# A two-layer streaming encoder step on one core: residuals written straight to SBUF, weight splits and norm rows in another order, another end

## The reference, cut to what matters

```
for each of 2 layers, for 256 prompt rows and 32 sample rows (288 tokens, D_MODEL 1024):
    mod = silu(c) @ w_mod + b_mod                  # shift, scale, gate for both norms
    h = rms_norm(x, g1) * (1 + scale1) + shift1
    merged = sum of 4 gated token mixers of h      # attention kinds, gMLP
    x = x + gate1 * (merged @ w_out)               # output projection, residual
    h = rms_norm(x, g2) * (1 + scale2) + shift2    # second norm
    up = h @ w_up ; conv over time, width 3        # 1024 -> 2 x 2816
    x = x + gate2 * ((silu(gate) * val) @ w_down)  # down projection, residual
y = rms_norm(x, final_g)                           # plus keys, values, conv states as outputs
```

## Time and profile before

| | us |
|---|---|
| median of 3 runs | 1148.5 (1146.59 to 1148.95) |
| profiled execution | 1147.06 |
| its span, first to last instruction | 1145.3 |
| TensorE busy | 1099.8 (96%) |
| GpSimd busy | 691.7 (60%) |
| ScalarE busy | 591.8 (52%) |
| VectorE busy | 537.6 (47%) |

### The profile page before, as it was taken

How to read it: one execution, slowest core, us unless ns; L and a number is a source line. 1 busy time by engine, 2 the same in 40 slices (tenths; PEclk the granted TensorE clock), 3 DMA queues, 4 the chain that set the end, 5 groups by cost and what they waited for, 6 DMA issues and landing times.

```text
span 1145.3 us, 23004 instructions
## 1 busy us (share of the span) xinstructions
PE 1099.8 (96%) x8298; PEld 1004.5 (88%) x8298; DVE 537.6 (47%) x1332; ACT 591.8 (52%) x1095; POOL 691.7 (60%) x310
## 2 busy tenths in 40 slices
PE   4899999999999899999999999999999989999996
PEld 0787888887999899999999788888899989999996
DVE  2547513456266744442246562355536675444212
ACT  1554544545446665565456444454544576566531
POOL 0454435445466787777878444444657678777882
PEclk8899999999999999999999999999999999999998
DMA  9855546756654254444566555574634425444451
GB/s 362 326 181 205 215 184 225 256 175 249 226 191 153 95 182 165 155 175 159 186 208 251 203 212 195 184 254 161 196 124 140 167 88 185 169 151 179 154 189 70
DMA packets 82110, 216.01 MB, mean 189 GB/s; under 512 B 9240, under 2 KB 29280, under 8 KB 81776
## 3 DMA queue, kind: packets, MB, share of 16 engines
q1 hardware_dynamic: 82032, 214.93, 53.6%
HBM read 209.85 MB, written 5.05 MB: 188 GB/s over the span
## 4 chain that ended last, share of the span: by engine, by line
PE 67%; issue 13%; POOL 9%; DMA 3%; DVE 3%; ACT 2%; SPq 2%; POOLq 0%; DVEq 0%; ACTq 0%
PE ps L681 13%; PE ps L683 13%; PE ps L682 13%; POOL wlo L582 8%; PE ps L707 8%; PE ps L708 7%; PE ps L709 7%; DMA raw<-stream 3%; PE ps L637 2%; POOL ol L600 1%; SPq L478 1%; ACT whi L1167 1%; PE ps L631 1%; DVE work L1638 0%; PE ps L852 0%
## 5 line engine op out<-in xcount | busy, mean ns | idle before, releaser
L582 POOL TENSOR_TENSOR wlo<-raw,whi 128x1024 fp32r<-128x1024 f32 x282 | 673.6, 2394 | 427.2 <-ACT whi L1167 327.0
L1167 ACT ACTIVATE whi<-raw 128x1024 fp32r<-128x1024 f32 x204 | 213.4, 1055 | 103.7 <-PE ps L683 62.4
L707 PE MATMUL ps<-hh,whi 128*128 128x288 f32 x864 | 264.0, 306 | 1.2 <-ACT gb L1255 0.6
L708 PE MATMUL ps<-hl,whi 128*128 128x288 f32 x864 | 256.0, 296 | 0.0
L709 PE MATMUL ps<-hh,wlo 128*128 128x288 f32 x864 | 255.5, 296 | 0.0
L681 PE MATMUL ps<-oh,whi 128*128 128x290 f32 (+1 forms) x816 | 244.9, 300 | 10.6 <-POOL ol L600 3.5
L683 PE MATMUL ps<-oh,wlo 128*128 128x290 f32 (+1 forms) x816 | 243.6, 299 | 0.0
L682 PE MATMUL ps<-ol,whi 128*128 128x290 f32 (+1 forms) x816 | 242.8, 298 | 0.0
L707 PEld LDWEIGHTS ps<-hh,whi 128*128 128x128 f32 x864 | 162.7, 188 | 38.9 <-issue 34.7
L681 PEld LDWEIGHTS ps<-oh,whi 128*128 128x128 f32 x816 | 155.2, 190 | 13.7 <-POOL ol L600 5.0
L708 PEld LDWEIGHTS ps<-hl,whi 128*128 128x128 f32 x864 | 163.0, 189 | 0.1
(11 more groups left out here) (258 smaller groups left out, 1593.7 us busy)
## 6 DMA issues: line engine op xcount, KB each, us to landing
raw<-stream SPq DMA_DIRECT2D x232, 512.0 KB, 4.3
mraw<-stream SPq DMA_DIRECT2D x40, 1024.0 KB
raw<-stream SPq DMA_DIRECT2D x88, 128.0 KB, 5.1
raw<-stream SPq DMA_DIRECT2D x24, 384.0 KB, 5.1
first<-mod_first SPq DMA_DIRECT2D x16, 512.0 KB, 11.0
raw<-stream SPq DMA_DIRECT2D x24, 256.0 KB, 5.3
o_proj<-proj SPq DMA_DIRECT2D x12, 288.0 KB
kvk<-keys_t SPq DMA_DIRECT2D x6, 512.0 KB, 3.9
```

The lines of the kernel that those rows point to most:

```text
L582: nc.gpsimd.tensor_tensor(wlo[:, slot, :], raw[:, slot, :], whi[:, slot, :].bitcast(F32), ALU.subtract).then_inc(lo_ready, 1)
L707: mm(out, whi[:, slot, w], high, start=(i == 0), stop=False)
L708: mm(out, whi[:, slot, w], low, start=False, stop=False)
L1167: A(whi[:, slot, :], raw[:, slot, :], ACT.Copy).then_inc(hi_ready, 1)
```

## The change

The residual is written to `x` in SBUF by `add_back` itself, and that frees the bank. ScalarE's square and `u` read `x`; `u_low` on VectorE first copies `x` to PSUM bank 6 and makes the low of `u` from there. In the output projection ScalarE makes a piece's high after the square and `u` of a tile instead of before, and loads its table of logarithm and exponential behind the fourth tile. At the second norm ScalarE makes the high of the seventh up piece ahead of its last copies of `h` (before: between the convolutions), and GpSimd takes two weight lows, three of `h`, one weight low, five of `h`. At the end the last square is not added by VectorE but by a second matmul, the final weight is multiplied by ScalarE, and VectorE makes four products of two tiles each.

```diff
-                q = lows_and_norm(Q_UP + AHEAD, 2, ((1, 0, 2), (1, 2, 5), (1, 5, KT)))
+                q = lows_and_norm(Q_UP + AHEAD, 2, ((2, 0, 3), (1, 3, KT)))
...
-            sum_squares(DEPTH, 1)
+            pe.wait_ge(squares_added, upto(DEPTH, squares_added, -1))
+            mm(ps[:, 7, 0:T], cst[:, C_ONE:C_ONE + P], work[:, 0, :], start=True, stop=False)
+            pe.wait_ge(squared, upto(DEPTH, squared, 0))
+            mm(ps[:, 7, 0:T], cst[:, C_ONE:C_ONE + P], work[:, KT - 1, :], start=False, stop=True).then_inc(sums_ready, 1)
...
+                def square(m, tile):
                     act.wait_ge(bank_free[tile % 2], taken(l, tile // 2 + 1))
                     A(work[:, m, :] if m else ps[:, 7, 0:T], x[:, m, :], ACT.Square).then_inc(squared, 1)
+                def u_high(n, m):
+                    u = oh if n == 1 else hh
+                    for g, (a, b, o) in enumerate(((0, TP, 0), (TP, T, TP + 2))):
+                        i = A(u[:, m, o:o + b - a], x[:, m, a:b], ACT.Copy, scale=norm_a[:, n - 1, m, g:g + 1])
+                    i.then_inc(uh_ready, 1)
...
-                exp_and_log()
+                high(Q_OUT + AHEAD)
                 act.wait_ge(merged_l, upto(l, merged_l))
                 u_shift(2)
                 for m in range(KT):
-                    high(Q_OUT + m + AHEAD)
-                    if m:
-                        square(2, m - 1, (m - 1) % 2, (0, TP))
-                square(2, KT - 1, (KT - 1) % 2, (0, TP))
-                high(Q_UP + AHEAD)
+                    square(m, OUT_TILE + m)
+                    u_high(2, m)
+                    high(Q_OUT + m + 1 + AHEAD)
+                    if m == 3:
+                        exp_and_log()
                 root(2)
...
                     shift_up(j)
-                    if j < 2:
-                        high(Q_UP + AHEAD + 1 + j)
+                    high(Q_UP + AHEAD + 1 + j)
                     norm_high(2, *UP_CHUNKS[j])
...
-                        q = Q_UP + 2 * p + g + AHEAD
-                        if q >= Q_UP + AHEAD + 3:
-                            high(q)
...
+                    square(m, DOWN_TILE + m)
                     if l + 1 < DEPTH:
-                        square(1, m, m % 2, (0, TP + 2))
+                        u_high(1, m)
                     else:
-                        last_square(m, DOWN_TILE + m)
+                        in_order(A(x[:, m, :], x[:, m, :], ACT.Copy, scale=fg[:, m:m + 1]))
...
+                def add_back(m, tile, gate_at, cols):
+                    for g, ((a, b), c) in enumerate(zip(((0, TP), (TP, T)), cols)):
+                        i = V.scalar_tensor_tensor(x[:, m, a:b], ps[:, tile % 2, c:c + b - a], mod[:, gate_at + m, g:g + 1],
+                                                   x[:, m, a:b], ALU.mult, ALU.add)
+                    i.then_inc(bank_free[tile % 2], 1)
+                def u_low(n, m, tile):
+                    dve.wait_ge(bank_free[tile % 2], taken(l, tile // 2 + 1))
+                    if m:
+                        dve.wait_ge(ul_ready, upto(l, ul_ready, (2 - n) * KT + m))
+                    in_order(V.tensor_copy(ps[:, 6, 0:T], x[:, m, :]))
...
-                        i = V.scalar_tensor_tensor(ul[:, m, o:o + b - a], ps[:, bank, c:c + b - a], norm_a[:, n - 1, m, g:g + 1],
+                        i = V.scalar_tensor_tensor(ul[:, m, o:o + b - a], ps[:, 6, a:b], norm_a[:, n - 1, m, g:g + 1],
                                                    uh[:, m, o:o + b - a].bitcast(F32), ALU.mult, ALU.subtract)
                     i.then_inc(ul_ready, 1)
-                    for g, ((a, b), c, o) in parts:
-                        i = V.tensor_copy(x[:, m, a:b], ps[:, bank, c:c + b - a])
-                    i.then_inc(bank_free[bank], 1)
...
-            for k in range(KT):
-                V.scalar_tensor_tensor(work[:, k, :], x[:, k, :], fg[:, k:k + 1], rstd[:], ALU.mult, ALU.mult).then_inc(y_ready, 1)
+            for k in range(0, KT, 2):
+                V.tensor_tensor(work[:, k:k + 2, :], x[:, k:k + 2, :], rstd[:].unsqueeze(1).broadcast_to([P, 2, T]),
+                                ALU.mult).then_inc(y_ready, 1)
```

More of the change, by code:

```diff
@@ L334, in encoder @@
         hl_ready = signal("hl_ready", 2 * KT)
-        residual = signal("residual", 2 * KT)
         uh_ready = signal("uh_ready", 2 * KT)
@@ L567, in _ @@
             for k in range(0, KT, 2):
-                sp.wait_ge(y_ready, k + 2)
+                sp.wait_ge(y_ready, k // 2 + 1)
                 sp.dma_start(y_fm[:, k:k + 2, :], work[:, k:k + 2, :]).then_inc(y_stored, 16)
@@ L1478, in up_tile @@
                     u = 2 * odd + g
-                    if r is None:
-                        q = Q_UP + 2 * p + g + AHEAD
-                        if q >= Q_UP + AHEAD + 3:
-                            high(q)
-                    else:
+                    if r is not None:
                         q = Q_UP + 2 * odd + 4 + g + AHEAD
@@ L1572, in add_square @@
                 dve.wait_ge(squares_added, upto(l, squares_added, at - 1))
-                V.tensor_tensor(work[:, 0, :] if k == KT - 1 else ps[:, 7, 0:T], ps[:, 7, 0:T], work[:, k, :],
+                last = KT - 1 if l < DEPTH else KT - 2
+                V.tensor_tensor(work[:, 0, :] if k == last else ps[:, 7, 0:T], ps[:, 7, 0:T], work[:, k, :],
                                 ALU.add).then_inc(squares_added, 1)
@@ L1667, in scale_tile @@
                     i.then_inc(in_scaled if t < Q_OUT else up_scaled, 1)
-                def add_back(n, m, bank, gate_at, cols):
-                    parts = list(enumerate(zip(((0, TP), (TP, T)), cols, (0, TP + 2))))
-                    for g, ((a, b), c, o) in parts:
-                        y = ps[:, bank, c:c + b - a]
-                        i = V.scalar_tensor_tensor(y, y, mod[:, gate_at + m, g:g + 1], x[:, m, a:b], ALU.mult, ALU.add)
-                    i.then_inc(residual, 1)
+                def add_back(m, tile, gate_at, cols):
[8 more added lines that the diff above has]
+                    in_order(V.tensor_copy(ps[:, 6, 0:T], x[:, m, :]))
                     if n == 2:
@@ L2028, in _ @@
                     dve.wait_ge(piece_done, upto(l, piece_done, done(Q_OUT + m)))
-                    add_back(2, m, m % 2, 16, (0, TP))
+                    add_back(m, OUT_TILE + m, 16, (0, TP))
+                    u_low(2, m, OUT_TILE + m)
                 for b in range(2):
@@ L2102, in _ @@
                     dve.wait_ge(piece_done, upto(l, piece_done, done(Q_DOWN + 3 * m + 2)))
+                    add_back(m, DOWN_TILE + m, 40, (0, TP + 2))
                     if l + 1 < DEPTH:
-                        add_back(1, m, m % 2, 40, (0, TP + 2))
-                    else:
-                        for g, ((a, b), c) in enumerate(zip(((0, TP), (TP, T)), (0, TP + 2))):
-                            i = V.scalar_tensor_tensor(x[:, m, a:b], ps[:, m % 2, c:c + b - a], mod[:, 40 + m, g:g + 1],
-                                                       x[:, m, a:b], ALU.mult, ALU.add)
-                        i.then_inc(bank_free[m % 2], 1)
+                        u_low(1, m, DOWN_TILE + m)
+                    elif m < KT - 1:
                         add_square(l + 1, 1, m)
```

## The result

The changed kernel takes 1139.2 us (median of 4 runs, 1138.62 to 1140.81), the kernel before 1147.88 in the same comparison (1146.59 to 1148.95): a ratio of 0.9925, 95% interval 0.9909 to 0.9941. The forecast was 1140.1. The profiled execution took 1138.62 us, its span is 1136.8, so 8.4 us less by the time and 8.5 by the span, where the sum said 8.4.

The account below looks back on a forecast made before the run. TensorE, busy nearly throughout, was taken as the bound, so only its waits could pay. 4.9 + 2.3 + 1.2 = 8.4 us off 1147.06 gave 1138.7, forecast as a median of 1140.1, range 1137.0 to 1145.0 (8 in 10).

Parts of the forecast that it names:

- the sum: Whole kernel: A, B and C together save 4.9 + 2.3 + 1.2 = 8.4 us.
- A: Output projection: the residual frees the bank early, removing TensorE's waits; 2 x 2.44 = 4.9 us.
- B: Second norm: the low-weight wait moves from seventh to eighth up tile; 1.17 us per layer, 2.3 in all.
- C: Program end: last square added by TensorE (0.5 us) and four products for eight (0.7): 1.2 us (1.0 to 1.25).
- The new order of residual, square and u has cover throughout: Down projection of layer 0: a tile lasts 8.9 us, so the new order was costed at nothing.
- (1): Second norm: the eighth up tile's wait takes all that the seventh's gives; 1142.4 us, chance 0.12.
- (3): Output projection: the third tile waits for a residual queued on VectorE, not the bank; A falls away, 1145.0, chance 0.05.
- (4): Output projection: VectorE's copy to PSUM waits for a GpSimd low in every tile; 22 us, about 1162, chance 0.04.
- (5): Second norm: TensorE's clock stays low for sixth to eighth up tiles, both layers; 12.6 us, 1152.7, chance 0.04.

Follow-up runs that it names:

- The square of kernels: Changed kernel with bank release behind the low of u (1141.47 us), with ScalarE's old order (1139.34 us), and with both (1143.65 us).
- experiment 5: Changed kernel with the high of the seventh up piece back at its old place, GpSimd's new order kept: 1144.11 us (10 runs).
- experiment 6: Changed kernel with GpSimd's old order at the second norm, the early high of the seventh up piece kept: 1139.05 us.
- experiment 7: Changed kernel with the eighth up piece's high moved from the loop to ahead of the fourth shift, and GpSimd's old order: 1138.18 us.
- old_low_order: The kernel of experiment 6: changed kernel with GpSimd's old order at the second norm, 1139.05 us.
- experiment 9: Changed kernel without the copy of x to PSUM, the low of u reading x in SBUF: 1139.41 us.

## Why the prediction was right, and where it was not

- **The sum** (8.4 against 8.5 by the span) is better than its terms, by luck: A, B and C together gave 7.9 us, and 0.5 came from scatter between the layers.
- **A** held in size (5.2 against 4.9; in the profile after the matmuls of this stage took 0.1337 us each, not 0.1347; with the 25.90 that some profiles have it would be 4.8). The chain that it named was the right one, but it gave the gain to the early release and costed ScalarE's new order as a harmless side effect. The square of kernels shows that either is enough for the wait at O2. With the new order the low of O0 ends at 348.10, 0.25 us before O2 starts: a release behind it would have done.
- **"The new order of residual, square and u has cover throughout"** in the down projection was wrong in its reason. A tile of 8.9 us looks like ample cover, but VectorE stood 6.1 us there until ScalarE's u came, and the old release had 0.7 us to spare. The early release is what makes this place safe; with a late one the third tile waited 1.2 to 1.3 us.
- **B** held in its order of events (the wait moves to U7, U6 waits for the third convolution) and in most of its size: U7 came 27.60 us after U0, 27.5 forecast; 1.9 us against 2.3. Most of what is missing went behind U7: from its first matmul to that of U8 it is now 3.34 us, 0.13 more than in the kernel before (3.21), where U7 ran on without a wait. The prediction counted such a restart for U6 before and not for U7 after. That it is the place of U6's high and not GpSimd's order that pays is shown by experiments 5 and 6. That the order pays nothing may hold only while U7's low is late: in the profile of experiment 7 the old order cost 1.5 us per layer behind an early U7, but the medians do not show it.
- **C** was mis-sized: 0.8 instead of 1.2 (1.0 to 1.25). The products gave 0.75 as costed (3.52 to 2.77). From the residual to the products it gave 0.38, not 0.5: TensorE gets the last square 0.43 us earlier (1.23 behind the residual instead of 1.67, although the square itself starts 0.06 later), and the logarithm follows the matmul 0.06 later. And the span ends 0.28 later behind the last product, which the sum left out: it took the end of the products for the end of the program. The three make 0.86; the last residual came 0.04 later behind D0. What makes the end 0.28 longer is open.
- **Rivals.** (1), (3) and (4) did not come: U7 gave time, O2 did not wait, the copy took 0.46 beside lows, every time. (5), the clock, did not come in the changed kernel, but a fall is real in this stage: it cost 1.4 us per layer in the profile of experiment 5. (The 2.6 us per tile that the prediction took for it follow from no row; 14 matmuls in 3.60 us make it 2.9.) The fear was aimed at the wrong side, though. The Trainium skill ("TensorE: Matmul & The Clock Gate", section "A second HAM failure mode: psum-queue depth-cycling", the one behind the section that the prediction names) has it that short idle times between groups of matmuls can make the clock swing. The traces here do not show that: the order that feeds U4 in small pieces, with waits up to 0.35 us, left it at 1.00, and the falls in this stage came behind single waits of 1.75 us and more.

What stays open: why the kernel before kept its clock behind waits of 1.75 and 2.28 us in layer 1, and old_low_order behind 1.75, while others fell behind waits as long.

## What to carry to other kernels

When a wait hangs on a chain, list every edit that shortens the chain before giving the gain to one of them; two sufficient edits look like one cause until they are undone in a square. Look for the idle time of an engine ahead of the late step: moving one copy of 1.06 us into an idle place of ScalarE gave 3.1 us by the stretches, where term B of the change gave 1.9. And an edit that is worth nothing today (an order hidden behind a later wait) may be worth keeping for the day when that wait goes.

## What the runs showed of the hardware

- VectorE's instructions with two SBUF inputs waited for the GpSimd low that ran, to its end. The subtraction of 128x16 starts beside a low three times in each of the 13 profiles; all 39 times it ended 0.03 to 0.04 us behind that low, after 0.28 to 1.96 us (1.94 to 1.96 in five kernels). The low of u of 128x256 read from SBUF took up to 2.68 us instead of 0.48 (experiment 9). The copy from SBUF to PSUM, with one SBUF input, took 0.46 us in each of its 24 places in every profile that has it. The Trainium skill says the same ("SBUF — State Buffer", section "SBUF: two separate sides": an exclusive lock, held for the whole instruction), and the traces agree.
- Behind a single wait TensorE's granted clock went to the 1.2 GHz level in both layers of two kernels (waits of 2.91 and 2.95, 1.76 and 1.78) and in layer 0 of two more (1.75 and 1.76), though the engine had been busy for over 9 of the 10 us ahead of the wait. In layer 1 of the latter two it did not. In the mixers it went there behind waits of 0.91 and 0.92 us (experiments 5 and 9). In the second norm such a wait cost up to 1.4 us per layer above its length.
